# Small experts' weight blocks in runs of four instead of three (hybrid encoder trunk, one core)

## The chip, the core and the metric

One NeuronCore of one Trainium2 chip runs the whole program. The metric is the device time in microseconds of one execution. Five engines work from their own instruction streams and meet at semaphores: TensorE (PE) multiplies, ScalarE (ACT) and VectorE (DVE) prepare operands and read results, GpSimd (POOL) does little here, SyncE (SP) issues the loads of weights. One SP queue carries all weight blocks of 1 MB; its DMAs finish in the order in which they are issued.

## The reference, cut to what matters

Two layers: attention of three kinds, then a channel mixer. The second layer's mixer is the part of this case, a top-2-of-8 expert SwiGLU over 256 tokens:

```python
def swiglu(x, w_gate, w_up, w_down):
    return (jax.nn.silu(x @ w_gate) * (x @ w_up)) @ w_down

def moe_swiglu(x, w_router, w_gate, w_up, w_down):
    logits = (x @ w_router).astype(jnp.float32)
    top_v, top_i = lax.top_k(logits, TOP_K)
    gates = jax.nn.softmax(top_v, axis=-1)
    ...
    for e in range(N_EXPERTS):
        out = out + combine[..., e:e + 1].astype(x.dtype) * swiglu(x, w_gate[e], w_up[e], w_down[e])
    return out
```

Each expert has three weights of 1024 x 3584 in float32, 42 blocks of 1 MB in all: 14 of gate, 14 of up, 14 of down. How many experts are used, and by how many tokens, is found at run time.

## The kernel before

An expert with over 32 tokens is *large*: it is computed for all 256 tokens, and each of its weight blocks is split by ACT (`w_hi`, L1013) and then DVE (`w_lo`, L1586) into two fp32r halves, so that PE does 24 matmuls of 128x512 per block, with the weights as the moving side. An expert with at most 32 tokens is *small*: its tokens are gathered (`xs`), and PE reads the float32 block where it landed, with four matmuls in four column groups of the array (L2297 for gate and up, L2307 for down). A profile shows each of these float32 matmuls as two records, so a small block is eight.

With this case's inputs two experts are large (L0, L1 below) and three small (S0, S1, S2); the other three take no token. So one pass over the list TRIO runs, 210 blocks long, and neither PAIR nor REST. `expert_units()` gives an expert's blocks in order: in chunk c (0 to 3) the gate blocks, then the up blocks (two each in chunk 0, four each in the others), then down 0 to 13. `interleaved()` mixes them: it lays the 84 large blocks in order and puts up to RUN small ones behind a large one when so many are due; after a small expert's last up or last down block a run ends, and the next large block has none behind it (`pause`). Below, S1u2.3 is small expert 1, up, chunk 2, part 3; S1d6 is its down block 6.

The order sets these things:

- **Loads.** `load_order()` moves a large block's load three large blocks ahead of its use. The loads go round a ring of seven buffers (six of `raw`, and `raw_last`). Load j waits on SP for the buffer of load j-7: a small block's comes free when PE has used it (`unit_used`), a large one's when DVE has split it (`lo_done`). A load that waits holds back all behind it.
- **Splits.** The three slots of `w_hi` and `w_lo` hold the next three large blocks. ACT splits block o+3 once PE has finished large block o (`large_split`).
- **Small results.** When the last gate (or up) block of a chunk is done, bank 6 (or 7) is read by ACT (L1034) and DVE (L1600, L1612); the transposes of the product (L2284) go to bank 5.
- **Small experts' outputs.** After down block 13 ACT copies the sum (L1072) and PE scatters it to the tokens (L2315): quarters 0 to 2 behind the next large block, quarter 3 behind the one after it. DVE adds each to `acc` (L1638). Quarters 2 and 3 go through bank 5. Bank 5 also takes the transposed selection matrix of the next small expert (L2222), behind that expert's block u0.1; `bank5_read()` makes PE wait there, ahead of block u0.1 itself, until DVE has added quarter 3 (semaphore `added`).

The mixing rule itself:

```python
        due = min(len(smalls) * (k - 1) / (len(larges) - 6), len(smalls))
        if done + RUN <= due or due == len(smalls):
            for unit in smalls[done:done + RUN]:
                if not pause:
                    order.append(unit)
                    pause = unit[2:] in (("up", NCH - 1, PARTS[-1] - 1), ("down", N_DOWN - 1, 0))
                    done += 1
```

Of the kernel before, what the change touches and what calls it, by code (L numbers as in the profile page):

```python
# [59 lines left out]

NR = 6
NRE = 7
RUN = 3
NH = 3
IDLE_BANK = 2
UNIT = 2048
# [27 lines left out]
def interleaved(n_l, n_s):  # L94
# [10 lines left out]
    for k, unit in enumerate(larges):  # L105
# [6 lines left out]
# [4 lines that stand above are left out]
# [2360 lines left out]
```

## Time and profile before

| | |
|---|---|
| median of 3 runs | 1117.65 us (1115.64 to 1119.57) |
| the profiled execution | 1118.47 us |
| its span | 1116.5 us |
| mean granted TensorE clock | 0.995 |
| PE busy | 1085.3 us, 97% |
| DVE busy | 620.4 us, 56% |
| ACT busy | 453.3 us, 41% |
| read from HBM | 301.55 MB |
| small blocks in PE records | 568 + 104 of L2297, 336 of L2307 |
| large gate and up blocks in PE records | 440 of L2271: 8 for each of 55 blocks |

The timeline lists for each engine when an instruction starts and how long it takes; matmuls overlap in it, so the time that one costs is the distance from its start to the next start. Where an instruction stood idle, the reason stands in brackets at its end. The expert stage runs from about 492 us to 1107 us of the span; two layer norms and the output store follow.

### The profile page before, as it was taken

How to read it: one execution, taken by the hardware profiler on the slowest of the kernel's cores; microseconds unless marked ns; L12 is line 12 of the kernel's file. 1: busy time of each engine (PE TensorE's matmuls, PEld its weight loads, DVE VectorE, ACT ScalarE, POOL GpSimd, SP SyncE). 2: the span in 40 equal slices, each digit the busy share in tenths (PEclk: the TensorE clock that was granted, in tenths of full speed). 3: DMA queues.
4: the chain of work that ended last, by engine and by line, in shares of the span. 5: the costliest groups of instructions: out<-in, count | busy, mean ns of one | idle time of the engine just before them, and what ended most of it. 6: DMA issues, size and time to landing. Idle time of an engine off the chain costs nothing.

```text
span 1116.5 us, 14414 instructions
## 1 busy us (share of the span) xinstructions
PE 1085.3 (97%) x5833; PEld 806.8 (72%) x5833; DVE 620.4 (56%) x698; ACT 453.3 (41%) x540; POOL 43.8 (4%) x45
## 2 busy tenths in 40 slices
PE   7899999999999999989999999999999999999996
PEld 6677878888887788866666767666675766667564
DVE  3887676777467876665444534543443445344325
ACT  4656543444335566243434343332333343433220
POOL 3000020000014000000000000000000000000001
PEclk9999999999999999999999999999999999999998
DMA  9943256555656712179999989899998989999872
GB/s 283 363 149 126 76 189 193 187 186 188 204 172 198 240 40 80 38 284 375 366 385 369 366 328 407 318 391 373 366 397 338 401 311 381 373 366 370 337 287 78
DMA packets 97995, 303.71 MB, mean 272 GB/s; under 512 B 5082, under 2 KB 7272, under 8 KB 97920
## 3 DMA queue, kind: packets, MB, share of 16 engines
q1 hardware_dynamic: 95520, 295.19, 71.4%
q0 software_dynamic: 2112, 6.87, 2.3%
q8 instruction: 50, 0.82, 0.3%
q10 hardware_dynamic: 288, 0.63, 0.1%
q14 instruction: 25, 0.20, 0.1%
HBM read 301.55 MB, written 1.12 MB: 271 GB/s over the span
## 4 chain that ended last, share of the span: by engine, by line
PE 84%; DVE 6%; DMA 4%; ACT 2%; issue 2%; DVEq 0%; POOL 0%; POOLq 0%; SPq 0%; ACTq 0%
PE bank L1758 19%; PE bank L1759 18%; PE bank L2271 9%; PE bank L2297 7%; PE bank L1858 6%; PE bank L1891 6%; PE bank L1897 3%; PE bank L2307 3%; PE bank L1958 2%; PE bank L2067 2%; DMA raw<-in_w_in 2%; PE bank L2052 1%; DMA raw<-in_moe_w_down 1%; PE bank L1984 1%; PE bank L2231 1%
## 5 line engine op out<-in xcount | busy, mean ns | idle before, releaser
L1586 DVE TENSOR_TENSOR w_lo<-raw,w_hi 128x2048 fp32r<-128x2048 f32 x73 | 167.4, 2293 | 250.8 <-ACT w_hi L1013 250.8
L1758 PE MATMUL bank<-w_hi,xT 128*128 128x512 f32 x620 | 251.0, 405 | 0.0
L1759 PE MATMUL bank<-w_hi,xT 128*128 128x512 f32 x620 | 242.5, 391 | 0.0
L1013 ACT ACTIVATE w_hi<-raw 128x2048 fp32r<-128x2048 f32 x73 | 139.7, 1914 | 245.1 <-PE bank L2271 151.3
L1146 DVE TENSOR_TENSOR w_lo<-raw,w_hi 128x2048 fp32r<-128x2048 f32 x62 | 141.9, 2290 | 63.1 <-ACT w_hi L823 62.9
L823 ACT ACTIVATE w_hi<-raw 128x2048 fp32r<-128x2048 f32 x64 | 122.6, 1918 | 109.5 <-PE bank L1897 50.5
L1758 PEld LDWEIGHTS bank<-w_hi,xT 128*128 128x128 f32 x620 | 116.5, 188 | 46.2 <-issue 15.4
L1759 PEld LDWEIGHTS bank<-w_hi,xT 128*128 128x128 f32 x620 | 116.6, 188 | 21.9
L1758 PE MATMUL bank<-w_hi,hT_hi 128*128 128x512 f32 x312 | 124.3, 398 | 0.0
L1759 PE MATMUL bank<-w_hi,hT_lo 128*128 128x512 f32 x312 | 121.8, 390 | 0.0
L2271 PE MATMUL bank<-w_lo,xT 128*128 128x512 f32 x440 | 118.0, 390 | 0.0
L2271 PEld LDWEIGHTS bank<-w_lo,xT 128*128 128x128 f32 x440 | 82.6, 188 | 17.9
L1858 PE MATMUL bank<-w_lo,hT_hi 128*128 128x512 f32 x312 | 83.5, 389 | 0.0
L1758 PEld LDWEIGHTS bank<-w_hi,hT_hi 128*128 128x128 f32 x312 | 58.6, 188 | 24.7 <-issue 10.7
L2297 PE MATMUL bank<-raw,xs 128*32 128x512 f32 x568 | 69.1, 598 | 0.1
L1891 PE MATMUL bank<-xT,w_hi 128*128 128x512 f32 x288 | 68.8, 391 | 0.0
L1858 PEld LDWEIGHTS bank<-w_lo,hT_hi 128*128 128x128 f32 x312 | 58.6, 188 | 12.5
L1759 PEld LDWEIGHTS bank<-w_hi,hT_lo 128*128 128x128 f32 x312 | 58.6, 188 | 11.5
L1891 PEld LDWEIGHTS bank<-xT,w_hi 128*128 128x128 f32 x288 | 53.0, 188 | 10.3
L1958 PE MATMUL bank<-w_lo,xT 128*128 128x512 f32 x192 | 52.3, 395 | 0.0
L780 POOL TENSOR_TENSOR rstd<-var_eps,tab 128x1 f32<-128x1 f32 x8 | 9.0, 1122 | 929.5 <-DVE var_eps L1315 929.5
L1586 DVE TENSOR_TENSOR w_lo<-raw_last,w_hi 128x2048 fp32r<-128x2048 f32 x10 | 22.9, 2292 | 39.4 <-ACT w_hi L1013 39.4
(253 smaller groups left out, 1218.0 us busy)
## 6 DMA issues: line engine op xcount, KB each, us to landing
raw<-in_moe_w_gate SPq DMA_DIRECT2D x60, 1024.0 KB, 9.0
raw<-in_moe_w_down SPq DMA_DIRECT2D x60, 1024.0 KB, 9.5
raw<-in_moe_w_up SPq DMA_DIRECT2D x59, 1024.0 KB, 8.0
raw<-in_w_in SPq DMA_DIRECT2D x23, 1024.0 KB, 10.7
raw<-in_ffn_w_gate SPq DMA_DIRECT2D x11, 1024.0 KB, 5.2
raw<-in_ffn_w_up SPq DMA_DIRECT2D x11, 1024.0 KB, 5.0
raw<-in_ffn_w_down SPq DMA_DIRECT2D x11, 1024.0 KB, 4.9
raw_last<-in_moe_w_up SPq DMA_DIRECT2D x11, 1024.0 KB, 8.3
```

The costliest lines, as they stand in the source:

```text
L823: nc.scalar.activation(w_hi[:, n % NH, :], raw[:, n % NR, :], ACT.Copy).then_inc(hi_done, 1)
L1013: nc.scalar.activation(w_hi[:, m % NH, :], block_buffer(j), ACT.Copy).then_inc(hi_done, 1)
L1146: nc.vector.tensor_tensor(w_lo[:, n % NH, :], raw[:, n % NR, :], w_hi[:, n % NH, :].bitcast(F32), ALU.subtract).then_inc(lo_done, 1)
L1586: nc.vector.tensor_tensor(w_lo[:, m % NH, :], block_buffer(load[at[o]]), w_hi[:, m % NH, :].bitcast(F32), ALU.subtract).then_inc(lo_done, 1)
L1758: nc.tensor.matmul(o, hi, wh, start=start, stop=False)
L1759: nc.tensor.matmul(o, lo, wh, start=False, stop=False)
L1858: ins = nc.tensor.matmul(bank[:, banks[2 * tt + ch], :], xh[:, 2 * i + k, t], wl[:, 2 * k + ch, :], start=False, stop=i == last and k == 1)
L1891: nc.tensor.matmul(bank[:, tile_bank(c, kind, j), :], wh[:, k, j * P:(j + 1) * P], xT[:, kt, :, :].rearrange("p h s -> p (h s)"), start=kt ...
L1897: ins = nc.tensor.matmul(bank[:, tile_bank(c, kind, j), 0:SEQ], wl[:, k, j * P:(j + 1) * P], xT_hi[:, kt, :], start=False, stop=kt == KT - 1)
L1958: ins = nc.tensor.matmul(o, xT_hi[:, kt, t], wl[:, k, :], start=False, stop=kt == KT - 1)
L2271: ins = nc.tensor.matmul(bank[:, 2 * tt + h, :], xT_hi[:, kt, t], wl[:, k, h * CW:(h + 1) * CW], start=False, stop=kt == KT - 1)
L2297: ins = nc.tensor.matmul(bank[g * SMALL:(g + 1) * SMALL, b, :], xs[:, part * (4 // nh) + g // nh, :], w[:, g, :], start=part == 0, stop=pa ...
```

## The change

One number: `RUN` goes from 3 to 4. It is read only in `interleaved()`, and what depends on it is the order of the blocks in TRIO (and PAIR) and, through `load_order()`, of their loads.

```diff
-RUN = 3
+RUN = 4
```

The blocks are the same 210. In TRIO there were 45 runs of small blocks (39 of three, three of two, three of one); now there are 33 (30 of four, three of two). Behind the runs stood one large block 12 times, two 32 times and four once; now one stands 4 times, two 14 times, three 13 times and four twice. Since a chunk has four gate and four up blocks, and chunk 0 has two and two, each run is now a whole sum; before, sums were broken over two runs. The order near the first scatter of quarter 3 is, before, `L0d2 S1g0.0 S1g0.1 S1u0.0 L0d3 S1u0.1 S1g1.0 S1g1.1`, and now `L0d3 S1g0.0 S1g0.1 S1u0.0 S1u0.1 L0d4 S1g1.0 ...`. Where L0 ends it is, before, `L0d13 S1u2.2 S1u2.3 S1g3.0 L1g0.0 S1g3.1 S1g3.2 S1g3.3 L1g0.1`, and now `L0d13 S1u2.0 ... S1u2.3 L1g0.0 S1g3.0 ... S1g3.3 L1g0.1`.

PE at S1's first blocks, behind the scatter of S0's quarter 3 (L2315). Before:

```order
L1858 MATMUL bank<-w_lo,hT_hi 128x512 x4
L2315 MATMUL bank<-up_s,tab 128x512 [waits rows_in,g_in,selT_in,added,s_in,y_in]
L2297 MATMUL bank<-raw,xs 32x512 [waits block_in6,g_in]
L2297 MATMUL bank<-raw,xs 32x512 x3
L2297 MATMUL bank<-raw,xs 32x512 [waits block_in0]
L2297 MATMUL bank<-raw,xs 32x512 x3
L2297 MATMUL bank<-raw,xs 32x512 [waits block_in1]
L2297 MATMUL bank<-raw,xs 32x512 x3
L1758 MATMUL bank<-w_hi,hT_hi 128x512 [waits hi_done]
```

Now, at the same place:

```order
L1858 MATMUL bank<-w_lo,hT_hi 128x512 x4
L2315 MATMUL bank<-up_s,tab 128x512 [waits rows_in,g_in,selT_in,added,s_in,y_in]
L2297 MATMUL bank<-raw,xs 32x512 [waits block_in0,g_in]
L2297 MATMUL bank<-raw,xs 32x512 x3
L2297 MATMUL bank<-raw,xs 32x512 [waits block_in1]
L2297 MATMUL bank<-raw,xs 32x512 x3
L2297 MATMUL bank<-raw_last,xs 32x512 [waits block_in2]
L2297 MATMUL bank<-raw_last,xs 32x512 x3
L2297 MATMUL bank<-raw,xs 32x512 [waits g_in,added,rows_in,block_in3,selT_in,s_in]
L2297 MATMUL bank<-raw,xs 32x512 x3
L2222 MATMUL bank<-tab 128x128 x2
```

The fourth small block, S1u0.1 with its wait on `added`, has moved from behind the next large block into the run. What DVE does there, split, addition of the quarter, reading of bank 6, is the same up to that point in both kernels:

```order
L1586 TENSOR_TENSOR w_lo<-raw,w_hi 128x2048 [waits hi_done]
L1676 TENSOR_LOAD work
L1676 ISA x2
L1638 ISA [waits scatter_psum,added]
L1638 SCALAR_TENSOR_TENSOR acc<-bank,comb,acc 128x512
L1600 TENSOR_TENSOR hid_s<-bank,hid_s 64x512 [waits s_half]
```

The addition stands behind the split of a large block in DVE's stream, in both.

ACT at the scatter of S1's quarter 3, which stood behind L1g2.2 and stands behind L1g2.3 now; L1060 is the SiLU of L1's gate sums, which follows L1g2.3. Before, from the copy of S1's output (L1072) on:

```order
L1072 ACTIVATE up_s<-bank 128x512
L1066 ACTIVATE hT_hi<-bank 128x4x128
L1013 ACTIVATE w_hi<-raw_last 128x2048
L1066 ACTIVATE hT_hi<-bank 128x4x128
L1013 ACTIVATE w_hi<-raw 128x2048
L1034 ACTIVATE hid_s<-bank 64x512
```

Now:

```order
L1072 ACTIVATE up_s<-bank 128x512
L1066 ACTIVATE hT_hi<-bank 128x4x128
L1013 ACTIVATE w_hi<-raw 128x2048
L1060 ACTIVATE row<-bank 128x1024
L1066 ACTIVATE hT_hi<-bank 128x4x128
L1060 ACTIVATE hid_last<-bank 128x1024
L1013 ACTIVATE w_hi<-raw 128x2048
L1034 ACTIVATE hid_s<-bank 64x512
```

The split whose second half precedes the addition on DVE now stands behind both SiLUs.

SP where L0 ends, from the load of S1u2.2 on. Before:

```order
L611 DMA raw<-in_moe_w_up 128x2x1024 [waits lo_done] x2
L611 ISA [waits unit_used]
L611 DMA raw_last<-in_moe_w_gate 128x2x1024
L611 DMA raw<-in_moe_w_up 128x4x512 [waits unit_used]
L611 ISA [waits unit_used]
L611 DMA raw<-in_moe_w_gate 128x2x1024
L611 ISA [waits lo_done]
L611 DMA raw<-in_moe_w_gate 128x2x1024
L611 ISA [waits lo_done]
L611 DMA raw<-in_moe_w_gate 128x2x1024
```

Now, from S1u2.3 on:

```order
L611 DMA raw<-in_moe_w_up 128x2x1024 [waits lo_done]
L611 DMA raw_last<-in_moe_w_up 128x4x512 [waits lo_done]
L611 ISA [waits lo_done]
L611 DMA raw<-in_moe_w_gate 128x2x1024
L611 ISA [waits lo_done]
L611 DMA raw<-in_moe_w_gate 128x2x1024
L611 ISA [waits unit_used]
L611 DMA raw<-in_moe_w_gate 128x2x1024
L611 ISA [waits unit_used]
L611 DMA raw<-in_moe_w_gate 128x2x1024
```

The last load in each is S1g3.3. Before, it waits for the split of L1u0.0 (the last `lo_done`), and S1g3.1 had been issued two waits earlier. Now S1g3.1 is the one that waits for the split of L1u0.0, and S1g3.2 and S1g3.3 stand behind it in the queue, waiting for the first two blocks of the run before.

## Rows read from the trace of the kernel before

**Rows 1.** The page: busy time of the engines; DMA share in 40 slices

```profile
PE 1085.3 (97%) x5833; PEld 806.8 (72%) x5833; DVE 620.4 (56%) x698; ACT 453.3 (41%) x540; POOL 43.8 (4%) x45
DMA  9943256555656712179999989899998989999872
```

**Rows 2.** The page: the chain that ended last, by engine

```profile
PE 84%; DVE 6%; DMA 4%; ACT 2%; issue 2%; DVEq 0%; POOL 0%; POOLq 0%; SPq 0%; ACTq 0%
```

**Rows 3.** Source view of L2297, a small expert's gate and up blocks

```profile
L2297 PE MATMUL bank<-raw,xs x568: 589/592/617, 510.1 to 1025.9; 128*32 128x512 f32 x190
L2297 PE MATMUL bank<-raw_last,xs x104: 592/592/617, 511.8 to 1012.8; 128*32 128x512 f32 x104
```

**Rows 4.** Windows: stretch, busy of PE, PEld, DVE, ACT, POOL; clock, DMA share, GB/s

```profile
660.00:760.00 100.00, 100.00 (x524) 67.91 (x517) 44.02 (x35) 32.26 (x27) 0.00 (x0) 1.00 0.96 372
```

**Rows 5.** Timeline of PE (start, duration, line, count): a run's edges

```profile
506.37 1.07 PE L2271 MATMUL bank<-w_lo,xT 128*128 128x512 f32 x4
507.28 0.39 PE L1758 MATMUL bank<-w_hi,xT 128*128 128x512 f32 x1
...
509.09 1.07 PE L2271 MATMUL bank<-w_lo,xT 128*128 128x512 f32 x4
510.09 1.93 PE L2297 MATMUL bank<-raw,xs 128*32 128x512 f32 x16
...
512.80 0.50 PE L1758 MATMUL bank<-w_hi,xT 128*128 128x512 f32 x1
513.13 0.39 PE L1759 MATMUL bank<-w_hi,xT 128*128 128x512 f32 x1
```

**Rows 6.** Timeline of PE: two small blocks apart

```profile
553.40 1.06 PE L2297 MATMUL bank<-raw,xs 128*32 128x512 f32 x8
...
555.14 1.04 PE L2297 MATMUL bank<-raw,xs 128*32 128x512 f32 x8
```

**Rows 7.** Timeline of PE: a scatter of one quarter, and what follows

```profile
710.57 1.12 PE L2315 MATMUL bank<-up_s,tab 64*128 64x512 f32 x2
711.63 2.78 PE L2297 MATMUL bank<-raw,xs 128*32 128x512 f32 x24
```

**Rows 8.** Timeline of ACT, then of DVE, behind that scatter

```profile
710.74 1.91 ACT L1013 ACTIVATE w_hi<-raw 128x2048 fp32r<-128x2048 f32 x1 [2.21 <-PE bank L1858]
...
712.68 2.29 DVE L1586 TENSOR_TENSOR w_lo<-raw,w_hi 128x2048 fp32r<-128x2048 f32 x1 [3.18 <-ACT w_hi L1013]
714.89 0.74 DVE L1638 SCALAR_TENSOR_TENSOR acc<-bank,comb,acc 128x512 f32<-128x512 f32 x1
```

**Rows 9.** PE and ACT behind the next scatter; ACT's SiLU, grouped by form

```profile
905.92 2.35 PE L2297 MATMUL bank<-raw,xs 128*32 128x512 f32 x20
...
905.03 1.91 ACT L1013 ACTIVATE w_hi<-raw 128x2048 fp32r<-128x2048 f32 x1 [2.21 <-PE bank L2271]
...
L1060 ACT ACTIVATE hid_last<-bank 128x1024 f32<-128x1024 f32 x6 | 6.2, 1026 | 9.8 <-PE bank L2271 9.8
```

**Rows 10.** Timeline of PE and DVE at L0's end; the chain there

```profile
790.01 1.07 PE L1858 MATMUL bank<-w_lo,hT_hi 128*128 128x512 f32 x4
...
799.40 3.09 PE L2297 MATMUL bank<-raw,xs 128*32 128x512 f32 x24
...
793.93 2.28 DVE L1586 TENSOR_TENSOR w_lo<-raw,w_hi 128x2048 fp32r<-128x2048 f32 x1
...
796.38 5.01 DMA raw<-in_moe_w_gate
```

**Rows 11.** Timeline of PE: down blocks for which it waited

```profile
859.32 1.92 PE L2307 MATMUL bank<-raw,hs 128*32 128x512 f32 x16
862.34 1.06 PE L2307 MATMUL bank<-raw,hs 128*32 128x512 f32 x8 [1.10 <-DMA raw<-in_moe_w_down]
...
1056.39 1.06 PE L2307 MATMUL bank<-raw,hs 128*32 128x512 f32 x8
1058.95 1.06 PE L2307 MATMUL bank<-raw,hs 128*32 128x512 f32 x8 [1.50 <-DMA raw<-in_moe_w_down]
```

## Prediction of what the change does

> **What bounds the kernel now.** First the page. PE is busy 97% of the span while DVE stands at 56% and ACT at 41% [rows 1], and the chain that ended last runs through PE for 84% [rows 2]. DVE's 6% and DMA's 4% in the chain say that PE is sometimes handed over late. The change touches the expert stage alone, so I read that stage next. The source view counts 568 + 104 = 672 records of gate and up blocks of small experts; at eight records for each block and 28 such blocks for each expert these are three small experts [rows 3], so TRIO is what runs. In a stretch of that stage PE is busy 100 of 100 us at the full clock of 2.4 GHz (granted clock 1.00), and the DMA engines have a share of 0.96 at 372 GB/s [rows 4]. So PE is the bound with a second resource just behind it. A reader should hold on to that: what makes the use of blocks less even has a price here.
>
> The timeline gives the unit costs. Four matmuls of a large block take 507.28 - 506.37 = 0.91 us, so its 24 take 5.44 [rows 5]. A small block takes (555.14 - 553.40) / 2 = 0.87 [rows 6]. When PE waits block by block, the blocks come 1058.95 - 1056.39 = 2.56 us apart [rows 11]; that is the rate of the queue, three times slower than a run uses them. A load whose buffer has just come free lands 5.0 us after its issue [rows 10].
>
> **a. Fewer runs: a gain.** At a run's edge there are three small costs. The four matmuls ahead take 1.00 instead of 0.91; three blocks take 512.80 - 510.09 = 2.71 instead of 2.61; the first matmul behind takes 0.33 instead of 0.23 [rows 5]. That is 0.29 for a run. There are 45 - 33 = 12 runs fewer: -3.5 us, all of it on PE and so on the path.
>
> **b. Transposes inside a run.** The transposes L2284 of a chunk stood three times at a run's end and stand inside one now, each with one more such edge. No row shows this alone; between 0 and 0.29 for each, I take half: +0.4 us.
>
> **c. Two waits for an addition.** Block u0.1 of S1 and S2 carries the wait on `added`. Before, a large block of 5.44 us lay between the scatter of quarter 3 and that block, and hid the chain. Now only three small blocks lie between. Take the scatter behind S0's output: PE begins it at 710.57 and the run at 711.63 [rows 7], and would reach the fourth block at 711.63 + 3 x 0.87 = 714.2. The addition is queued on DVE behind the split of a large block: ACT starts it at 710.74, DVE at 712.68, and the addition runs from 714.89 for 0.74 [rows 8]. It ends at 715.6, and with 0.1 us for the semaphore PE resumes at 715.7: +1.5 us. These DVE rows do not depend on what PE does in the run, and behind the waiting matmul all of PE is queued.
>
> At the next such place the run starts at 905.92 and wants its fourth block at 908.5, and ACT's half of the split begins at 905.03 [rows 9]. There the order now puts the SiLU of L1's gate sums ahead of it, 1.03 us for the half that needs the block just finished [rows 9]. So w_hi runs from 906.1 to 908.0, w_lo (2.29) to 910.3, the addition to 911.0: +2.5 us. Both together: +4.0. The least that I can defend is 2.5, if DVE gets to the additions sooner by one small operation each; the most is 5.
>
> **d. Where L0 ends.** L0d13 ends at 790.9 (790.01 + 0.91); call that T. DVE first adds two quarters of L0, so the split of L1u0.0 runs from 793.93 to 796.2, and the load that it frees is issued at 796.38 = T + 5.5 and lands at 801.4 = T + 10.5 [rows 10]. Before, that load was S1g3.3, the last of its run, and the run took 3.09 instead of 2.78: a wait of 0.3. Now four small blocks follow L0d13 (3.5 and edges), then L1g0.0 (5.44), so PE wants S1g3.0 to S1g3.3 at T + 9.3, 10.2, 11.1 and 11.9. The load which that split frees is S1g3.1 now. S1g3.2 and S1g3.3 wait for buffers that are free long before, but they are queued behind it on SP. They land at T + 10.5, 13.1 and 15.7. PE waits 15.7 - 11.9 = 3.8, against 0.3 before: +3.5 us. Bounds: 0 if the splits come early enough, 5 if S1g3.0 is late too.
>
> [...]
>
> **e. Elsewhere: the ring of seven.** A stretch of one run and the large blocks behind it costs PE the small blocks x 0.87 + 0.3 + the large ones x 5.44, and the queue 2.56 for each. Three and one: 8.4 against 10.2. Three and two: 13.8 against 12.8. Four and one: 9.2 against 12.8. Four and two: 14.7 against 15.4. Four and three: 20.1 against 17.9. So stretches in which the queue falls behind were 12, each by 1.9, and will be 4 by 3.6 and 14 by 0.7; the ring covers one such debt when it was full before. PE now waits at two places of this kind: (862.34 - 859.32) - 2 x 0.87 = 1.3, and 2.56 - 0.87 = 1.7 [rows 11]; 3.0 together. No row says what the new order makes of it. One bound is that both go (-3.0); the other is that two debts of 3.6, at L0d4 and L1u2.0, are paid in full on top (+7). I take +2, nearer to the lower, because at just these two places PE has waited under c and the queue has used that time.
>
> **Sum.** -3.5 + 0.4 + 4.0 + 3.5 + 2.0 = +6.4 us. On the profiled execution of 1118.47 us that is 1124.9; it stands 0.8 above the median of 1117.65, on which the forecast is **1124.0 us**. Operand splits, SiLUs and reads are as many as before; their engines have the room (56% and 41%), and I cost them at nothing except where c names them.
>
> **The rivals.**
> - *The ring fills up behind three large blocks* (the other side). 13 runs are followed by three large blocks, where the queue gains 2.2 us. If that surplus is what decides, d costs nothing and the waits of today vanish: -3.5 + 0.4 + 4.0 - 3.0 = -2.1, 1115.5 us. For it: the slices with DMA at 9 leave no idle queue to gain from, but those at 8 do [rows 1]. Against it: seven buffers hold no more than seven blocks, so beyond that the surplus is idle queue, not stock. It decides from the point where no run finds fewer than four landed blocks.
> - *Waits only move.* c stands, and d and e add up to nothing: +0.9, 1118.6 us. For it: every wait of PE gives the queue time, so 4 us under c may pay for later blocks.
> - *The queue becomes the bound.* Debts add up, because the queue already runs at a share of 0.96 [rows 4] and every microsecond it idles behind a full ring is lost: e is +7 and not +2, 1129.0 us.
> - That the change does not do what it says is out: the order of blocks is computed, and a block fewer or more would show at once.
>
> **How the numbers follow.** Chances: the forecast 0.55, the ring fills 0.10, waits only move 0.18, the queue is the bound 0.17. A measurement of this kernel can tell about 0.3% from no change, 3.4 us. Slower by more than that means above 1121.0: all of the queue's case and nearly all of the forecast's, 0.72. Faster means below 1114.3: less than half of the first rival, 0.05. The rest is 0.23. Range 1118.4 to 1129.8: it takes in the bounds of d and most of e, and most of the case of waits that only move.
>
> **What would show it.** PE's L2297 at S1u0.1 and S2u0.1 would show idle time ended by DVE's L1638, 1.5 and 2.5 us; if there is none, c is wrong. The run S1g3 behind L1g0.0 should show records of eight, 2.56 us apart, ended by the DMA of gate blocks. The records of L2297 and L2307 should stand in 33 runs and the busy time of PE be nearly as before, with more idle time. If the waits for DMAs in down blocks (L2307) grow beyond 3 us, e was too small; if they are gone, the surplus behind three large blocks is real. What would make the forecast wrong as a whole is d: it rests on one place and on SP's order.

## The result, and the profile after

| | before | after |
|---|---|---|
| median | 1118.15 us (6 runs, 1115.64 to 1119.74) | 1125.08 us (6 runs, 1123.45 to 1127.94) |
| ratio to the kernel before | | 1.0065, interval 1.0052 to 1.0078 |
| the profiled execution: span | 1116.5 us | 1123.1 us |
| mean granted TensorE clock | 0.995 | 0.988 |

The change makes the kernel slower by 6.9 us; the forecast was 1124.0 us (+6.4), range 1118.4 to 1129.8. The spans of the two profiled executions differ by 6.6 us. The page of after, with engines' busy time, the granted clock and the DMA share in 40 slices, and the chain (as [rows 1] and [rows 2]):

```profile
span 1123.1 us, 14414 instructions
PE 1087.5 (97%) x5833; PEld 812.4 (72%) x5833; DVE 620.2 (55%) x698; ACT 452.5 (40%) x540; POOL 43.8 (4%) x45
PE   7999999999999999999999999999899999999996
PEclk9999999999999999989999999999899999999998
DMA  9943266555647612189999999799889979999972
...
PE 81%; DMA 7%; DVE 6%; ACT 3%; issue 2%; SPq 0%; POOL 0%; POOLq 0%; DVEq 0%; ACTq 0%
```

PE's busy time has hardly moved, and its share of the chain fell from 84% to 81% while DMA's rose from 4% to 7%. The 29th slice (786 to 814 us) is new: PE and the clock both stand at 8 in it. The clock's other new digit, the 18th (477 to 505 us), lies before the expert stage and costs nothing: the lower clock fills time in which PE of the kernel before stands waiting there, and in both kernels the first run of correction matmuls (L2271) begins at 495.22. What counts is read from the waits. PE's own waits in the expert stage, after (engine, line waited for: us in total, times, longest):

```profile
PE bank L2297 <- DMA raw<-in_moe_w_gate: 5.7, 4, 1.5
PE bank L2297 <- DVE acc L1638: 3.8, 2, 2.3
PE bank L2297 <- DMA raw_last<-in_moe_w_gate: 0.7, 1, 0.7
PE bank L2307 <- DMA raw<-in_moe_w_down: 0.3, 1, 0.3
```

and before:

```profile
PE bank L2307 <- DMA raw<-in_moe_w_down: 2.6, 2, 1.5
```

Before, PE waited only for down blocks. Now it waits for gate blocks, and twice for DVE's addition. The tables of waits leave out what weight loads waited and what the lower clock cost, so I took each run of small blocks by the distance from its first matmul to the first matmul of the next large block. Undisturbed runs of four take 3.57 us (2.71 for three, 1.85 for two); those with the transposes L2284 inside take 4.07 to 4.10, the two with the gather of the next expert's tokens 4.94. All runs that took longer than their kind:

| run, after | took | undisturbed | more |
|---|---|---|---|
| 566.6, S0g2 | 4.43 | 3.57 | 0.9 |
| 717.0, S1g0 to S1u0.1 | 5.45 | 3.76 with L2222 | 1.7 |
| 728.1, S1g1 | 5.06 | 3.57 | 1.5 |
| 800.2, S1g3 | 8.00 | 3.57 | 4.4 |
| 917.6, S2g0 to S2u0.1 | 6.31 | 3.76 with L2222 | 2.6 |
| 929.6, S2g1 | 5.24 | 3.57 | 1.7 |
| 1085.6, S2d12 and d13 | 2.39 | 1.85 | 0.5 |

Before, there were three: 799.4 (0.3), 859.3 (1.3) and 1055.3 (1.9).

**The waits for the addition** (c). PE at S1's first run, then DVE there:

```profile
715.90 1.12 PE L2315 MATMUL bank<-up_s,tab 64*128 64x512 f32 x2
716.96 1.92 PE L2297 MATMUL bank<-raw,xs 128*32 128x512 f32 x16
718.70 1.04 PE L2297 MATMUL bank<-raw_last,xs 128*32 128x512 f32 x8
721.22 1.07 PE L2297 MATMUL bank<-raw,xs 128*32 128x512 f32 x8 [1.48 <-DVE acc L1638]
```

```profile
718.01 2.29 DVE L1586 TENSOR_TENSOR w_lo<-raw,w_hi 128x2048 fp32r<-128x2048 f32 x1 [3.20 <-ACT w_hi L1013]
720.22 0.75 DVE L1638 SCALAR_TENSOR_TENSOR acc<-bank,comb,acc 128x512 f32<-128x512 f32 x1
```

The fourth block would have started at 716.96 + 3 x 0.87 = 719.6 and starts at 721.22, when the addition behind the split has ended (720.22 + 0.75). At S2's first run, ACT, DVE and PE:

```profile
916.68 1.02 ACT L1060 ACTIVATE hid_last<-bank 128x1024 f32<-128x1024 f32 x1 [1.70 <-PE bank L2271]
917.60 1.90 ACT L1013 ACTIVATE w_hi<-raw 128x2048 fp32r<-128x2048 f32 x1
```

```profile
919.53 2.29 DVE L1586 TENSOR_TENSOR w_lo<-raw,w_hi 128x2048 fp32r<-128x2048 f32 x1 [3.83 <-ACT w_hi L1013]
921.74 0.75 DVE L1638 SCALAR_TENSOR_TENSOR acc<-bank,comb,acc 128x512 f32<-128x512 f32 x1
```

```profile
922.74 1.06 PE L2297 MATMUL bank<-raw,xs 128*32 128x512 f32 x8 [2.34 <-DVE acc L1638]
```

The SiLU of 1.02 us stands ahead of the split, and the wait is longer by about that: the two runs took 1.7 and 2.6 us more.

**L0's end** (d), with the matmuls of the large block behind the run:

```profile
800.18 2.09 PE L2297 MATMUL bank<-raw,xs 128*32 128x512 f32 x16
803.75 1.06 PE L2297 MATMUL bank<-raw,xs 128*32 128x512 f32 x8 [1.49 <-DMA raw<-in_moe_w_gate]
806.32 1.93 PE L2297 MATMUL bank<-raw,xs 128*32 128x512 f32 x8 [1.50 <-DMA raw<-in_moe_w_gate]
808.18 0.80 PE L1758 MATMUL bank<-w_hi,xT 128*128 128x512 f32 x1
808.78 0.63 PE L1759 MATMUL bank<-w_hi,xT 128*128 128x512 f32 x1
...
811.76 1.23 PE L2271 MATMUL bank<-w_lo,xT 128*128 128x512 f32 x4
812.83 0.39 PE L1758 MATMUL bank<-w_hi,xT 128*128 128x512 f32 x1
```

The third and the fourth block start late: 803.75 - 801.92 = 1.8 and 806.32 - 804.62 = 1.7 us, 3.5 of waits. The last block then takes 808.18 - 806.32 = 1.9 instead of 0.97, and from 808.78 to 811.76 matmuls start 0.43 apart instead of 0.23. The windows view has the clock of that stretch (last columns: clock, DMA share, GB/s):

```profile
800.00:820.00 20.00, 17.01 (x78) 10.33 (x77) 4.77 (x3) 6.13 (x6) 0.00 (x0) 0.83 1.03 412
```

In finer windows the granted clock leaves 1.00 at about 805.2, inside the second wait, and is back at about 812.0: some 7 us at 1.2 GHz. It is the only fall in the rest of the stage: from 505 to 800 and from 813 to 1112 us the granted clock is 1.00. That the late matmuls are slow by the clock is read from their spacing and this column; what brought the clock down is an inference from the order of events. The low clock costs 0.9 us in the run and 812.83 - 808.18 = 4.65 instead of 2.88, 1.8 us, behind it: 2.7 us that no term of the prediction had.

**A debt elsewhere** (e), the run behind the first wait for the addition:

```profile
728.06 2.78 PE L2297 MATMUL bank<-raw,xs 128*32 128x512 f32 x24
732.12 1.06 PE L2297 MATMUL bank<-raw,xs 128*32 128x512 f32 x8 [1.28 <-DMA raw<-in_moe_w_gate]
```

### The profile page after: what moved, and what is told of

Its sections match the earlier page's. It is cut to its first block, busy times and chain, and to the rows that moved or that the text cites. A ratio compares the mean times of both kernels' runs of the same rounds, so it can differ in the third digit from the quotient of the medians.

```text
span 1123.1 us, 14414 instructions
## 1 busy us (share of the span) xinstructions
PE 1087.5 (97%) x5833; PEld 812.4 (72%) x5833; DVE 620.2 (55%) x698; ACT 452.5 (40%) x540; POOL 43.8 (4%) x45
## 4 chain that ended last, share of the span: by engine, by line
PE 81%; DMA 7%; DVE 6%; ACT 3%; issue 2%; SPq 0%; POOL 0%; POOLq 0%; DVEq 0%; ACTq 0%
PE bank L1758 19%; PE bank L1759 18%; PE bank L2271 8%; PE bank L1891 6%; PE bank L1858 6%; PE bank L2297 5%; PE bank L1897 3%; PE bank L2307 3%; DMA raw<-in_moe_w_gate 3%; PE bank L1958 2%; PE bank L2067 2%; PE bank L2052 1%; DMA raw<-in_w_in 1%; DMA raw_last<-in_moe_w_gate 1%; PE bank L1984 1%
## 5 line engine op out<-in xcount | busy, mean ns | idle before, releaser
L1586 DVE TENSOR_TENSOR w_lo<-raw,w_hi 128x2048 fp32r<-128x2048 f32 x70 | 160.4, 2292 | 244.9 <-ACT w_hi L1013 244.9
L1013 ACT ACTIVATE w_hi<-raw 128x2048 fp32r<-128x2048 f32 x70 | 133.9, 1913 | 219.9 <-PE bank L2271 138.8
L1146 DVE TENSOR_TENSOR w_lo<-raw,w_hi 128x2048 fp32r<-128x2048 f32 x62 | 141.8, 2288 | 63.3 <-ACT w_hi L823 63.2
L823 ACT ACTIVATE w_hi<-raw 128x2048 fp32r<-128x2048 f32 x64 | 122.5, 1915 | 108.3 <-PE bank L1897 50.6
L1758 PEld LDWEIGHTS bank<-w_hi,xT 128*128 128x128 f32 x620 | 118.1, 190 | 42.6 <-issue 19.6
L1759 PEld LDWEIGHTS bank<-w_hi,xT 128*128 128x128 f32 x620 | 118.4, 191 | 22.7
L2271 PE MATMUL bank<-w_lo,xT 128*128 128x512 f32 x440 | 118.0, 390 | 0.0
L2271 PEld LDWEIGHTS bank<-w_lo,xT 128*128 128x128 f32 x440 | 82.9, 188 | 17.7
L1858 PE MATMUL bank<-w_lo,hT_hi 128*128 128x512 f32 x312 | 83.5, 389 | 0.0
L2297 PE MATMUL bank<-raw,xs 128*32 128x512 f32 x592 | 72.5, 604 | 9.6 <-DMA raw<-in_moe_w_gate 5.7
L1858 PEld LDWEIGHTS bank<-w_lo,hT_hi 128*128 128x128 f32 x312 | 58.6, 188 | 12.3
L1586 DVE TENSOR_TENSOR w_lo<-raw_last,w_hi 128x2048 fp32r<-128x2048 f32 x13 | 29.8, 2292 | 45.8 <-ACT w_hi L1013 45.8
L2297 PEld LDWEIGHTS bank<-raw,xs 128*32 128x32 f32 x592 | 15.7, 109 | 47.9 <-issue 34.3
```

What stands on the lines that cost most here:

```text
L823: nc.scalar.activation(w_hi[:, n % NH, :], raw[:, n % NR, :], ACT.Copy).then_inc(hi_done, 1)
L1013: nc.scalar.activation(w_hi[:, m % NH, :], block_buffer(j), ACT.Copy).then_inc(hi_done, 1)
L1146: nc.vector.tensor_tensor(w_lo[:, n % NH, :], raw[:, n % NR, :], w_hi[:, n % NH, :].bitcast(F32), ALU.subtract).then_inc(lo_done, 1)
L1586: nc.vector.tensor_tensor(w_lo[:, m % NH, :], block_buffer(load[at[o]]), w_hi[:, m % NH, :].bitcast(F32), ALU.subtract).then_inc(lo_done, 1)
L1758: nc.tensor.matmul(o, hi, wh, start=start, stop=False)
L1759: nc.tensor.matmul(o, lo, wh, start=False, stop=False)
```

## The experiments

Each ran beside the kernel before on the same chip. Since each trace is of one execution, and the work ahead of the expert stage varies from one to the next by up to 4 us, the traces are compared by the stage alone: from PE's first L2271 to the start of its last four L1858 (the same matmuls, whatever their line numbers in a run).

| kernel | runs | median | stage in its trace |
|---|---|---|---|
| before | 45 | 1118.15 | 610.56 |
| after | 33 | 1125.08 | 617.22 |
| 1, additions first | 33 | 1123.75 | 615.56 |
| 2, one run moved | 33 | 1120.90 | 612.93 |
| 3, L0's end alone | 45 | 1124.88 | 615.15 |
| 4, before, half loads | 45 | 1114.07 | 606.94 |
| 5, after, half loads | 33 | 1115.11 | 607.33 |
| 6, the same, additions first | 33 | 1110.39 | 603.22 |
| 7, runs of two, half loads | 63 | 1123.13 | 615.82 |

The theory: the change loses because its longer runs reach blocks that have not landed, at L0's end above all, and the waits for the addition are only partly a cost of their own. The rivals are in the expectations.

**1. Additions first.** In DVE's `run_units` the small experts' quarters are added ahead of the split:

```diff
-                    add_outputs(u)
+                    add_outputs(u, "L")
...
+                    add_outputs(u + 1, "S")
                     if u in at[0:-AHEAD]:
                         large_split(at, load, at.index(u) + AHEAD, off, off_l)
```

> The changed kernel, but DVE adds a small expert's quarters ahead of the split of a large block behind the same block, instead of behind it. The changed kernel stood 6.9 us above the kernel before, and its trace has two waits for the addition, 1.5 and 2.3 us. If these waits are a cost of their own (term c of the prediction), they vanish and the time falls by 3.8 to 4.2 us, to +2.9 against the kernel before. Rival: the queue of loads is behind at these places anyway, and the wait only stands in for a later one: the waits for DVE go, the next runs (S1g1 and S2g1) wait for their blocks by as much more (3 us or more each instead of 1.5), and the time stays at +6.9 (within 1). I hold the rival the likelier one, 0.6.

Measured: 1123.75 us, ratio 1.0046 (1.0032 to 1.0061), so 1.3 us less than the changed kernel (the two intervals overlap; the stage is 1.7 us shorter) beside 4.2 us of waits removed. No wait for DVE's addition is left in PE's waits. The wait for gate blocks is larger (5.7 before this edit; matmuls of small blocks have line 2298 here):

```profile
PE bank L2298 <- DMA raw<-in_moe_w_gate: 8.0, 6, 2.7
```

and the run of S1g1 shows where it went:

```profile
729.60 1.93 PE L2298 MATMUL bank<-raw,xs 128*32 128x512 f32 x16
731.86 1.07 PE L2298 MATMUL bank<-raw,xs 128*32 128x512 f32 x8 [0.34 <-DMA raw<-in_moe_w_gate]
734.41 1.06 PE L2298 MATMUL bank<-raw,xs 128*32 128x512 f32 x8 [1.49 <-DMA raw<-in_moe_w_gate]
```

That run takes 5.81 us instead of 5.06, S2g1 6.15 instead of 5.24, and the run at L0's end 9.04 instead of 8.00. So 2.7 of the 4.2 us came back in runs whose blocks were late, and 4.2 - 2.7 = 1.5 is about what the median and the stage show. Neither theory holds alone; the rival is nearer: the queue was behind, and the wait for DVE had given it time.

**2. One run moved away from L0's end.**

```diff
+TRIO = moved(TRIO, [("S", 1, "up", 2, part) for part in range(4)], ("L", 0, "down", 11, 0))
```

`moved` takes the four blocks out of the order and puts them behind the block named last.

> The changed kernel, but the run S1u2.0 to S1u2.3 stands behind L0d11 instead of behind L0d13, so that at L0's end no two runs have only one large block between them. In the changed kernel's trace the run S1g3 there takes 8.0 instead of 3.6 us, and the matmuls behind it ran for 4.7 us at the lower clock (1.2 GHz). If term d is right and the clock fell because of it, both go: 3.2 us of waits and 2.7 of clock, 5 to 6 us less, +1 to +2 against the kernel before, and granted clock 1.00 in the stretch from 800 to 820 us. Rival, the debt is the ring's and not this place's: the waits come up elsewhere (the run moved, or the next), and only the clock's part is won, +4 to +5.

Measured: 1120.90 us, ratio 1.0027 (1.0013 to 1.0041): 4.2 us less than the changed kernel (4.3 in the stage), between the two expectations. The run of S1g3 is undisturbed, and the clock of the stretch is back at full:

```profile
800.00:820.00 20.00, 20.00 (x104) 14.27 (x105) 7.67 (x5) 8.05 (x7) 0.00 (x0) 1.00 0.92 350
```

But the moved run now finds its last block late:

```profile
780.32 1.07 PE L2305 MATMUL bank<-raw,xs 128*32 128x512 f32 x8
784.70 1.06 PE L2305 MATMUL bank<-raw,xs 128*32 128x512 f32 x8 [1.06 <-DMA raw<-in_moe_w_up]
```

It takes 5.37 instead of 4.10 us with its transposes. So of the 5.9 us that sat at L0's end (4.4 more in the run, 1.8 of clock behind it, less 0.3 that stood there before), 1.3 came back at once. One placement of one run is more than half of what the change costs.

**3. That place alone, in the kernel before.** Runs of three as before, but at L0's end the eight blocks as in the changed kernel:

```diff
+TRIO = moved(TRIO, [("S", 1, "up", 2, part) for part in range(4)], ("L", 0, "down", 13, 0))
+TRIO = moved(TRIO, [("S", 1, "gate", 3, part) for part in range(4)], ("L", 1, "gate", 0, 0))
```

> The kernel before (runs of three), with one part of the change alone: where L0 ends, all of S1u2.0 to S1u2.3 stand behind L0d13 and all of S1g3.0 to S1g3.3 behind L1g0.0, as in the changed kernel. If place d is a cost by itself, S1g3.2 and S1g3.3 land late as in the changed kernel (two waits of 1.5 us), the clock falls to 1.2 GHz behind them and the kernel is 5 to 6 us slower than the kernel before, slightly more than what moving one run away won (4). If the clock stays up, +3. Rival: it took the runs of four before it to bring the queue behind; with runs of three up to there the waits are under 1 us and so is the difference.

Measured: 1124.88 us, ratio 1.0061 (1.0037 to 1.0085). The interval is wide: the seven executions run from 1122.20 us at a granted clock of 0.992 to 1130.49 at 0.987, and the profiled one is the fastest. Its stage is 4.6 us longer than that of the kernel before. PE at that run:

```profile
797.83 1.92 PE L2306 MATMUL bank<-raw,xs 128*32 128x512 f32 x16
802.28 1.06 PE L2306 MATMUL bank<-raw,xs 128*32 128x512 f32 x8 [2.53 <-DMA raw<-in_moe_w_gate]
804.84 1.94 PE L2306 MATMUL bank<-raw,xs 128*32 128x512 f32 x8 [1.50 <-DMA raw<-in_moe_w_gate]
806.71 0.80 PE L1767 MATMUL bank<-w_hi,xT 128*128 128x512 f32 x1
```

The same two late blocks, 2.7 and 1.7 us, without any longer run before L0's end; matmuls behind start 0.43 apart again. The run takes 8.88 instead of 3.57 us. The place is a cost by itself, and the rival falls. How much of it is the clock differs: here the low clock ends at 808, in the trace of the changed kernel at 812.

**4 and 5. Half loads of the small blocks, before and after.** In `expert_block`, for small experts only:

```diff
+                if half:
+                    nk = src.shape[1]
+                    to = block_buffer(j).rearrange("p (k n) -> p k n", k=nk)[:, 0:nk // 2, :]
+                    sp.dma_start(to, src[:, 0:nk // 2, :]).then_inc(block_in[j % NRE], 16)
+                    return
```

> The kernel before, but each small expert's block loads only its first half (512 KB); the rest of its buffer is whatever the block before it left there. So the queue has 126 x 0.5 MB less to bring, and the same number of instructions runs. Expected: the waits of PE for down blocks (3.2 us) go and nothing else, 3 us less than the kernel before. If the queue cost more than its waits show, it is 5 us or more less.

Measured: 1114.07 us, ratio 0.9960 (0.9946 to 0.9974), 4.2 us less than the kernel before, between the two expectations; the stage is 3.6 us shorter, about the 0.3 + 1.3 + 1.9 = 3.5 us by which the kernel before was late. These kernels load only the first half of each small block and compute with what lies in the rest of the buffer, so they are for timing alone; a half load also lands sooner by itself (3.6 us after its issue where the buffer has just come free, not 5.0), so they relieve the queue and shorten the single load together. The queue has room (compare the DMA row of [rows 1]):

```profile
DMA  9944265555655713167766668577676857676652
```

> The changed kernel with the same half loads of small blocks. The queue has room, so only what is not the queue's is left of the change: 12 run edges fewer (-3.5 to -4.2 us) and the two waits for the addition (+3.9). If that is so, this stands within 1 us of the kernel before with half loads, where with full loads the difference is 6.9; and PE shows the two waits on DVE's addition, 1.5 and 2.3 us, and none for a DMA, and the clock stays up. Rival: if this stands 3 us or more above the other, something besides the queue costs, and the account is wrong.

Measured: 1115.11 us, ratio 0.9974 (0.9963 to 0.9985). With full loads the two kernels stand 6.9 us apart, with half loads 1.0. PE's waits for small blocks:

```profile
PE bank L2303 <- DVE acc L1644: 3.8, 2, 2.3
PE bank L2303 <- DMA raw<-in_moe_w_gate: 0.5, 2, 0.3
```

So 5.9 of the 6.9 us hang on the loads: the blocks that come late, and the clock that falls with them (in this trace it stays at 1.00 there). The waits for the addition are there as before, and the edges saved pay for them. The 0.5 us for blocks were not expected: they are at L0's end again, where even half loads come late and the run takes 4.47 instead of 3.57.

**6. Half loads, additions first.** Experiments 1 and 5 together:

> The changed kernel with half loads of small blocks, and with the small experts' additions ahead of the splits. With full loads putting them first won only 1.5 to 2 us, since the waits moved to blocks. With room in the queue nothing should take their place: 3.8 to 4.2 us less than the changed kernel with half loads (1115.1), so 1111, which is also below the kernel before with half loads (1114.1) by the run edges saved, 3 to 4 us. Rival: if it wins 2 us or less here too, the wait for the addition is covered by something else than the queue.

Measured: 1110.39 us, ratio 0.9922 (0.9897 to 0.9947), 4.7 us less than number 5. What PE still waits for in small blocks:

```profile
PE bank L2304 <- DMA raw<-in_moe_w_gate: 0.5, 1, 0.5
```

With room in the queue the wait for the addition is worth all of its 4.2 us; with the queue full, 1.3. Against number 4 this kernel has 12 runs fewer. It is 3.7 us faster, by the medians and in the stage, and that although its run at L0's end takes 4.63 instead of 3.57, 1.1 more. So 12 edges are worth 4.8 to 4.9 us, 0.41 each. The two medians together are uncertain by some 3 us; the stages are one execution each, but it is their runs, one by one, that bear the figure out.

**7. Runs of two, with half loads.** `RUN = 2`, 63 runs:

> RUN = 2 with half loads of small blocks, nothing else changed: it prices a run's edge by itself, with no wait for blocks. The kernel before with half loads has 45 runs and stands at 1114.1. By the rows (0.29 us for an edge; 0.35 with the slower matmuls behind it) each further run costs that: with 18 to 22 more runs 5 to 8 us more, 1119 to 1122. If the difference is under 3 us, the gain that the change makes by having fewer runs is smaller than the prediction's term a.

Measured: 1123.13 us, ratio 1.0043 (1.0029 to 1.0057), 9.1 us above number 4 for 18 more runs, and 8.9 in the stage; 5 to 8 were expected. This order has a wait of its own, in which PE stands for ACT's copy of the gathered rows:

```profile
PE bank L2222 <- ACT xg L1024: 1.2, 2, 0.6
```

The two runs concerned take 3.57 instead of 1.85 + 1.06 = 2.91 us, 1.3 together. That leaves 7.6 us for 18 edges, 0.42 each: more than the 0.29 to 0.35 expected, and what experiment 6 gives. Stretches without waits or transposes show the same price. In this kernel a run of two and one large block behind it take 770.50 - 762.94 = 7.56 us:

```profile
762.94 1.92 PE L2303 MATMUL bank<-raw,xs 128*32 128x512 f32 x16
770.50 1.92 PE L2303 MATMUL bank<-raw,xs 128*32 128x512 f32 x16
```

In the kernel before, three and two take 567.23 - 553.40 = 13.83, and after the change four and two take 1076.40 - 1061.73 = 14.67. With 5.44 for a large block, each further small block in a run adds 0.84, and 0.43 to 0.44 is left for the run itself. So I take 0.42.

**8 and 9. Runs placed by when their blocks land.** The list names the large block (counted from 0) behind which a run stands, and its length; the first of the two:

```diff
+RUNS = [(3, 4), (6, 5), (9, 3), (11, 4), (14, 6), (17, 3), (19, 3), (21, 5), (24, 4), (27, 5), (30, 4), (33, 5), ...]
...
+        order.extend(next(smalls) for _ in range(counts.get(k, 0)))
```

> The runs of small blocks are placed by a list: 31 runs of two to six blocks, each put behind that large block at which, by the durations of the trace (0.87 and 5.44 us for a block on PE, 2.56 for one in the queue, 5.0 from a freed buffer to the landing), its blocks have landed. If the change lost because its runs meet late blocks and not because they are long, longer runs in the right places win what they save in edges and the waits of today: 14 edges fewer than the kernel before at 0.29 to 0.38 (-4 to -5 us) and up to 3.2 us of waits, 1110 to 1113. Rival: runs of five and six find late blocks wherever they stand, and the time is that of the kernel before or above.

Measured: 1113.82 us, ratio 0.9955 (0.9939 to 0.9971): faster by 4.2 us, but not the 1110 to 1113 expected.

```profile
span 1110.6 us, 14414 instructions
DMA  9943256555656712179999998899999999999952
```

DMA stands at 9 through nearly the whole stage, and PE itself waits for no small block. From its first L2271 to its last matmul PE takes 1106.85 - 495.22 = 611.6 us in the kernel before and 1095.55 - 493.74 = 601.8 here: 9.8 us less. That is what was promised, 14 edges at 0.42 and the 3.5 us of late blocks, 9.4 together. But the span is only 5.9 us shorter, because the end of the kernel has grown. Before:

```profile
1105.78 1.07 PE L1858 MATMUL bank<-w_lo,hT_hi 128*128 128x512 f32 x4
1108.67 1.29 DVE L1312 BATCH_NORM_STATS2 stats<-acc 128x6 f32<-128x512 f32 x2
```

and here, where line numbers are 16 higher:

```profile
1094.43 1.12 PE L2331 MATMUL bank<-up_s,tab 64*128 64x512 f32 x2
1096.79 1.29 DVE L1328 BATCH_NORM_STATS2 stats<-acc 128x6 f32<-128x512 f32 x2 [0.26 <-DVE acc L1654]
1102.85 1.29 DVE L1328 BATCH_NORM_STATS2 stats<-acc 128x6 f32<-128x512 f32 x2
```

The list puts S2's last run behind large block 80 of 0 to 83, so the scatter of S2's quarter 3 is now PE's last work, and both of the last layer norms stand behind it; in the kernel before the first of them (from 1102.61) ran beside the last large block. The second one starts 7.3 us after PE's end instead of 1.8. So 5.5 of the 9.8 us went to the order of the last few blocks.

> A second such list (31 runs of two to five), with the small experts' additions ahead of the splits of large blocks, so that a run may hold S1u0.1 without waiting for DVE. Expected 1110 to 1113 as the other list; if putting the additions first is worth something once the queue is in time, it is 1 us or more below it, else equal within 1 us.

Measured: 1114.77 us, ratio 0.9966 (0.9953 to 0.9979), also above the 1110 to 1113 expected. It is 0.95 us above the first list and the intervals overlap. The two lists differ as well, so this says little of the additions; no gain of them shows. This list has the same last run and the same end: S2's scatter is PE's last work.

Both are faster than the kernel before and than the changed one: longer runs do pay, where their blocks have landed. How the gain divides between run length and placement stays open; no run placed runs of three or four in this way. That an earlier last run would win the 5.5 us back is not shown either.

## Why the prediction was right, and where it was not

- **The bound.** PE with the queue just behind: right. Half loads alone won 4.2 us on the kernel before and took 5.9 of the 6.9 us off the change.
- **a, fewer runs.** -3.5 us was predicted at 0.29 for an edge. Experiments 6 and 7 give 0.41 and 0.42: -5.0. The step had the four matmuls ahead right (0.09). It compared the run with blocks of 0.87, but a further block in a run adds only 0.84, so a run of three holds 2.71 - 3 x 0.84 = 0.19 of edge and not 0.10; and the whole first half block behind is slower, by 0.14, not its first matmul alone.
- **b, transposes.** +0.4 was predicted. The three L2284 cost +0.4 (0.50 inside a run, 0.37 at its end), but L2222, which stood inside a run, stands at its end now (0.19 instead of 0.51, three times: -1.0), and the gather inside runs of four costs 1.37 instead of 1.06, twice: +0.6. About +0.1 together. Moving from inside to an end is the same edge with the other sign, and the step looked at one kind of transposes only.
- **c, the addition.** +4.0 was predicted at 1.5 and 2.5; the runs took 1.7 and 2.6 more. Mechanism, place and size right. That it is a cost of its own was wrong: it is worth 4.7 us when the queue has room and 1.3 as the kernel stands (experiments 6 and 1).
- **d, L0's end.** The late blocks were predicted at 3.8 us and came to 3.5, at the place and in the run named, S1g3.2 and S1g3.3 as said. Two small errors met there. The last block came at 806.3, T + 16.0, not 15.7 (T is 790.3 here); and PE reached the run at T + 9.9, not 9.3, because the run of S1u2 ahead holds the transposes L2284 (4.10 us), which the step left out. Missing altogether was the clock: 2.7 us more, for which the sum had no term. Less the 0.3 of before, d is +5.9 instead of +3.5.
- **e, elsewhere.** +2 was predicted. The runs of after lost 0.9 + 1.5 + 1.7 + 0.5 = 4.6, those of before 1.3 + 1.9 = 3.2: +1.4. The waits of before did go, as one bound had it, but two new ones stand in the run right behind each wait for the addition, where the prediction held that the queue would have used the time.
- **The sum.** -5.0 + 0.1 + 4.2 + 5.9 + 1.4 = +6.6 against 6.7 between the stages of the two traces. The mechanism stands: fewer edges gain, and c, d and e cost more than that. But that +6.4 came so near is partly luck. The gain of a was too small by 1.5 us and b and e were too high by 0.9, while d was too low by 2.4 for want of the clock; these errors cancel.
- **The page of the Trainium skill** (DMA: Bandwidth & Descriptors, section Anatomy of one DMA — SWDGE (gpsimd) path) gives about 2.0 us fixed plus the bytes at 436 GB/s, for transfers that GpSimd issues. Taken over to the loads here, which SP issues, that would be an estimate of 4.4 us for a block alone and 2.4 behind another, and of 2.8 us for the two late blocks. They were 3.5, and blocks come 806.32 - 803.75 = 2.57 apart. The trace's own rates were the better ones.
- **The rivals.** "Waits only move" is true of one part: 2.7 of c's 4.2 us do (experiment 1). "The ring fills up behind three large blocks" is false for this order, and experiments 8 and 9 show that another order comes near it. "The queue becomes the bound" did not come at the price named.

## What to carry to other kernels

When two resources are both near full, an order is judged by where its bursts fall: find the place at which two bursts stand close together and work out, load by load, when each can be issued and when it lands; one such place cost more here (5.9 us) than the twelve edges saved (5.0). A wait taken away in front of a resource that is behind comes back further down, so test it once with that resource relieved, and once as it is. And do not leave a unit's gain to one size for all bursts: placed one by one, runs of up to six blocks beat both kernels. Compare the stage as well as the span: the placed order won 9.8 us in the stage and lost 5.5 of them again behind it.

## What the runs showed of the hardware

- TensorE's granted clock fell from 2.4 to 1.2 GHz at L0's end, in the changed kernel nowhere else from 505 us on. There it fell inside the second of two waits of 1.8 and 1.7 us with 0.9 us of small blocks between them; in experiment 3 at the end of the second of waits of 2.7 and 1.7 us; in experiment 1 already 0.7 us behind the first of waits of 2.9 and 1.7. It stayed low for 7, 3 and 7 us, for a loss of up to 2.7 us (clock 0.83 over 20 us). It did not fall at single waits of 1.5 to 2.6 us elsewhere in the changed kernel, nor in the run at 729.6 of experiment 1, with idle times of 0.34 and 1.49 us. The Trainium skill (TensorE: Matmul & The Clock Gate, section Part 1: The HAM clock gate) describes the two levels, and this trace shows both.
- A run of small blocks (weight tiles of 128*32) between large blocks (128*128) costs PE 0.41 to 0.44 us beyond its blocks, in and out together, spread over the matmuls on both sides. That it is the change of tile shape that costs this is likely, but no run changed the shape alone.
